# A ninth lasting place for expert weights, and a gather by slot rows with transposes, in a one-core decoder block

## The reference

```python
h = rmsnorm(x, g_pre_ffn) * (1.0 + sc2) + sh2          # (256, 2048)
_, gsel = top_k(h @ w_group + b_group, 1)
pe = softmax((h @ w_router + b_router).reshape(T, 4, 8)[chosen group])
topv, topi = top_k(pe, 2)                              # two experts a token
for every expert e:                                    # w_gate, w_up (2048, 512), w_down (512, 2048)
    hid = silu(h @ w_gate[e]) * (h @ w_up[e])
    y = y + (hid * cw[:, e]) @ w_down[e]
x = x + gt2 * rmsnorm(y, g_post_ffn)
```

## Time and profile before

| | |
|---|---|
| median of 3 runs | 1552.59 us (1552.22 to 1553.93) |
| profiled execution: time, span | 1551.45 us, 1549.6 us |
| PE, DVE, ACT, POOL busy | 97%, 46%, 19%, 3% of the span |
| DMA engines, mean rate over the span | 381 GB/s |
| granted TensorE clock, mean | 0.996 of full speed |

### The profile page before, as it was taken

How to read it: one execution, slowest core, us unless ns; L and a number is a source line. 1 busy time by engine, 2 the same in 40 slices (tenths; PEclk the granted TensorE clock), 3 DMA queues, 4 the chain that set the end, 5 groups by cost and what they waited for, 6 DMA issues and landing times.

```text
span 1549.6 us, 19402 instructions
## 1 busy us (share of the span) xinstructions
PE 1509.9 (97%) x7980; PEld 811.3 (52%) x7980; DVE 714.8 (46%) x1289; ACT 289.9 (19%) x520; POOL 39.8 (3%) x57
## 2 busy tenths in 40 slices
PE   5999999999999999999999999999999999999996
PEld 2888888855654446344344444434434434434432
DVE  3574767676887636243233333332332332432325
ACT  2100311121332303111111112112012112112113
POOL 1001000000001200000000000000000000000003
PEclk9999999999999999999999999999999999999998
DMA  9999777799878996999999999999999999999994
GB/s 363 396 385 367 265 261 283 268 360 353 319 277 314 363 411 250 401 405 425 429 428 427 430 429 427 430 429 427 428 429 428 429 428 428 428 429 428 428 429 194
DMA packets 102802, 589.96 MB, mean 381 GB/s; under 512 B 6224, under 2 KB 16944, under 8 KB 77408
## 3 DMA queue, kind: packets, MB, share of 16 engines
q1 hardware_dynamic: 100384, 580.93, 92.4%
q0 software_dynamic: 1696, 5.66, 1.1%
q10 hardware_dynamic: 672, 2.66, 0.4%
HBM read 587.07 MB, written 2.16 MB: 380 GB/s over the span
## 4 chain that ended last, share of the span: by engine, by line
PE 82%; DMA 14%; DVE 2%; issue 0%; ACTq 0%; SPq 0%; ACT 0%; DVEq 0%
PE bank L1092 24%; DMA ring<-in_w_up 12%; PE bank L1203 11%; PE bank L930 7%; PE bank L646 7%; PE bank L1064 6%; PE bank L680 5%; PE bank L1084 5%; PE bank L871 4%; DMA ring<-in_w_ada 2%; PE bank L714 2%; PE bank L693 1%; PE bank L696 1%; DMA ring<-in_w_in 1%; PE bank L1100 1%; PE bank L837 1%
## 5 line engine op out<-in xcount | busy, mean ns | idle before, releaser
L1092 PE MATMUL bank<-ring,RN 128*64 128x512 f32 x1520 | 333.8, 593 | 3.7 <-DMA ring<-in_w_up 3.6
L1092 PEld LDWEIGHTS bank<-ring,RN 128*64 128x64 f32 x1520 | 108.4, 137 | 221.4 <-issue 208.7
L1203 PE MATMUL bank<-ring,RN 128*64 128x512 f32 x992 | 219.7, 595 | 1.0 <-issue 1.0
L1203 PEld LDWEIGHTS bank<-ring,RN 128*64 128x64 f32 x992 | 68.9, 137 | 137.8 <-issue 136.0
L2219 DVE COPY RG<-bank 64x512 f32<-64x512 f32 x64 | 44.1, 689 | 194.9 <-PE bank L1203 187.2
L1064 PEld LDWEIGHTS bank<-RN,RX 128*128 128x128 f32 x976 | 111.5, 192 | 13.0 <-issue 13.0
L1064 PE MATMUL bank<-RN,RX 128*128 128x128 f32 x976 | 115.7, 277 | 0.0
L930 PE MATMUL bank<-ring,RT 128*128 128x512 f32 x256 | 113.0, 596 | 0.8 <-DVE RT L2000 0.8
L1084 PE MATMUL bank<-RG,RN 128*128 128x512 f32 x240 | 109.5, 599 | 0.0
L2149 DVE TENSOR_SCALAR RN<-bank,aff 128x128 f32<-128x128 f32 x256 | 87.3, 403 | 47.6 <-PE bank L1064 45.7
L2205 DVE TENSOR_TENSOR RN<-bank,RN 128x512 f32<-128x512 f32 x32 | 22.1, 691 | 179.5 <-PE bank L1092 179.5
(11 more groups left out here) (387 smaller groups left out, 1488.0 us busy)
## 6 DMA issues: line engine op xcount, KB each, us to landing
ring<-in_w_down SPq DMA_DIRECT2D x64, 2048.0 KB, 15.5
ring<-in_w_up SPq DMA_DIRECT2D x63, 2048.0 KB, 21.0
ring<-in_w_ada SPq DMA_DIRECT2D x32, 2048.0 KB, 10.8
ring<-in_w_gate SPq DMA_DIRECT2D x32, 2048.0 KB, 19.7
ring<-in_w_in SPq DMA_DIRECT2D x18, 2048.0 KB, 9.3
RH<-in_w_gate SPq DMA_DIRECT2D x16, 2048.0 KB, 21.8
RT<-in_w_gate SPq DMA_DIRECT2D x16, 2048.0 KB, 18.9
ring<-in_w_ada SPq DMA_DIRECT2D x48, 512.0 KB, 11.7
```

The source lines that it names most:

```text
L1092: last = mm(bank[n // 2][c:c + CAP, :], tokT[:, k, q * CAP:(q + 1) * CAP], w[:, i, :], start=k < 2, stop=k >= KT - 2, skip_group_check=True)
L1203: last = mm(bank[2 + n % 2][64 * (n // 2):64 * (n // 2) + 64, :], hidT[:, k * CAP:(k + 1) * CAP], wdn[:, n * BLK:(n + 1) * BLK], start=k = ...
```

## The change

It does two things together.

1. **Memory.** `RN`, `RG[:, 1, :]`, `wide` and `RG[:, 0, :]` become parts of one tile `body`, side by side, so that the last 1024 columns of `RN`, `RG1` and `wide` are one place of 4096 columns. It is the third entry of `ODD`, for piece 2 of odd experts, for the whole loop. `AHEAD` now holds piece 3 of expert 1. Routing numbers move to the constants' tile and to `vec`, the recurrent heads' outputs to `RT[:, 8:16]`. The broadcast of the gate row moves from POOL's queue to SP's, after the third piece of the last expert is used.
2. **The gather.** `gather_rows(p, m)` takes `onehot` as weights and 512 columns of `x_t` as the moving operand, which leaves a bank with slots on the partitions. ACT copies the bank to one row buffer `slot_rows`, `gathered_T(p, m)` transposes it with four transposes into another bank, and DVE's `tokens` reads that. Expert 1's pair is still gathered in the old form.

The diff, cut to its core:

```diff
-        ODD = [blocks_of(RT[:, 0:KT, :].rearrange("p a b -> p (a b)")), blocks_of(RH[:, :])]
+        ODD = [blocks_of(RT[:, 0:KT, :].rearrange("p a b -> p (a b)")), blocks_of(RH[:, :]), blocks_of(body[:, 4096:8192])]
...
+        ROWS_BANK, TOKEN_BANK = [4, 5, 6, 7], [4, 5, 6, 4]
...
-            for s in (1, 0, 2, 4, 3, 5):
+            for s in (1, 0, 2):
+                first_piece(s)
             wait(sp, "rows_sent", 16 * 8)
             wait(sp, "x_permuted1")
...
+            first_piece(4)
+            wait(sp, "gate2_out", 16)
+            sp.dma_start(odd[2], expert_halves(1)[2]).then_inc(sig("odd_landed2").sem, 16)
+            for s in (3, 5):
+                first_piece(s)
+            used(sp, ("out", 3, 1))
...
+            sp.wait_ge(sig("expert_used").sem, (NE - 1) * HB + 3)
+            sp.dma_start(RG1[:, :], late_rows[3 * KT:4 * KT, :].rearrange("(o k) p -> o (k p)", o=1).to_broadcast([P, D]))\
+                .then_inc(sig("gain2_in").sem, 16)
...
+            def gather_rows(p, m):
+
+                if m == 3:
+                    pe.wait_ge(sig("ohwT_copied").sem, p + 1)
+                for tt in range(TT):
+                    last = mm(bank[ROWS_BANK[m]][:, :], onehot[:, tt, :], x_t[:, tt, m * BLK:(m + 1) * BLK], start=tt == 0, stop=tt == TT - 1)
+                last.then_inc(sig("rows_gathered").sem, 1)
+
+            def gathered_T(p, m):
+
+                pe.wait_ge(sig("rows_in_slots").sem, p * 4 + (m + 1))
+                if m == 3:
+                    pe.wait_ge(sig("gathered_used").sem, p * 4 + 5)
+                for j in range(4):
+                    last = tr(bank[TOKEN_BANK[m]][:, j * P:(j + 1) * P], slot_rows[:, j * P:(j + 1) * P], ident)
                 last.then_inc(sig("gathered").sem, 1)
...
-                        for m in range(3):
-                            gather_part(p + 2, m)
-                    if q == 1:
+                        for m in range(2):
+                            gather_rows(p, m)
                         pe.wait_ge(sig("ohw").sem, p + 1)
...
+                        gather_rows(p, 2)
...
                     if q == 1:
-                        gather_part(p + 2, 3)
+                        gathered_T(p, 0)
+                        gather_rows(p, 3)
+                        gathered_T(p, 1)
...
                         if k % 2 == 1:
                             last.then_inc(sig("expert_used").sem, 1)
+                            if q == 1:
+                                gathered_T(p, 2 + k // 2)
...
+            def slots_in(p, m):
+
+                act.wait_ge(sig("rows_gathered").sem, p * 4 + (m + 1))
+                if m:
+                    act.wait_ge(sig("gathered").sem, p * 4 + (m + 4))
+                fn(slot_rows, bank[ROWS_BANK[m]][:, :], ACT.Copy).then_inc(sig("rows_in_slots").sem, 1)
...
-                    if q == 1 and gather_next:
-                        tokens(p + 2, range(3))
...
-                        tokens(p + 2, range(3, 4))
+                        tokens(p + 2, range(4), TOKEN_BANK)
```

More of the change, by code:

```diff
@@ L499, in _, with first_pieces @@
             sp.dma_start(odd[0], expert_halves(1)[0]).then_inc(sig("odd_landed0").sem, 16)
-            def first_halves(e, q):
+            def first_pieces(e, q):
                 pieces = expert_halves(e + 2)
-                for s in range(2):
+                for s in range(3):
                     sp.wait_ge(sig("expert_used").sem, e * HB + (s + 1))
@@ L1053, in _, with gather_last_part @@
             keep_clock(8, 7)
[L1056 to L1062, removed]
+            def gather_last_part():
+                wait(pe, "gathered_used", 1)
+                for k in range(12, 16):
                     for tt in range(TT):
-                        last = mm(bank[GB[m % 3]][:, (k % 4) * P:(k % 4 + 1) * P], x_t[:, tt, k * P:(k + 1) * P],
+                        last = mm(bank[GB[0]][:, (k % 4) * P:(k % 4 + 1) * P], x_t[:, tt, k * P:(k + 1) * P],
                                   onehot[:, tt, :], start=tt == 0, stop=tt == TT - 1)
+                last.then_inc(sig("gathered").sem, 1)
+            def gather_rows(p, m):
[10 more added lines that the diff above has]
+                    last = tr(bank[TOKEN_BANK[m]][:, j * P:(j + 1) * P], slot_rows[:, j * P:(j + 1) * P], ident)
                 last.then_inc(sig("gathered").sem, 1)
@@ L1155, in pair @@
                     for n in range(4):
-                        if n == 2 and ahead:
+                        if n == 3 and ahead:
                             wait(pe, "ahead_landed", 16)
[L1158 to L1161, removed]
+                        elif n == 3 and first:
+                            wait(pe, "expert_landed3", 16)
+                        elif n == 3:
+                            pe.wait_ge(sig("expert_landed3").sem, e * 16)
                         elif q == 0:
@@ L1165, in pair @@
                             pe.wait_ge(sig(f"odd_landed{n}").sem, p * 16 + 16)
-                        w = AHEAD if ahead and n == 2 else ODD[n] if q == 1 and n < 2 else ring[:, n, :, :]
+                        w = AHEAD if ahead and n == 3 else ODD[n] if q == 1 and n < 3 else ring[:, n, :, :]
                         for m in range(2):
@@ L1493, in _ @@
             second_norm(0)
-            wait(act, "rows_sent", 16 * 8)
             x2T_copies(0)
@@ L1520, in expert_act @@
                 fn(sil[64:128, :], hid[0:64, :], ACT.Silu).then_inc(sig("silu").sem, 1)
+                if q == 1 and not last:
+                    slots_in(p, 0)
                 if q == 1:
@@ L1526, in expert_act @@
                    ACT.Copy).then_inc(sig("half_copied").sem, 1)
+                if q == 1 and not last:
+                    for m in range(1, 4):
+                        slots_in(p, m)
                 act.wait_ge(sig("expert_used").sem, e * HB + (5 if last else 6))
@@ L2142, in onehot_pair, with tokens @@
                 last.then_inc(sig("onehot").sem, 1)
-            def tokens(n, ms=range(4)):
+            def tokens(n, ms, banks):
                 for m in ms:
@@ L2163, in _ @@
             step(v.reduce_sum(rt[:, 200:201], rt[:, 0:64], AX), "over_counted")
-            tokens(1, range(3, 4))
+            tokens(1, range(3, 4), FIRST_BANK)
             for tt in range(TT):
```

121 lines of the change are left out of this document (58 added, 63 removed).

## The result

| | before | after |
|---|---|---|
| median of 4 runs each | 1552.4 us (1551.03 to 1553.93) | 1578.54 us (1577.36 to 1579.73) |
| profiled execution: time, span | 1551.45 us, 1549.6 us | 1579.73 us, 1577.5 us |

The ratio is 1.0169, with a 95% interval from 1.0156 to 1.0182: the change costs 26.1 us. Forecast were 1582 us and a range from 1570 to 1592.

The account below looks back on a forecast made before the run. PE's own work plus 5.4 us of weight waits was taken to bound the expert stage. Fifteen pairs at +2.31 us (+34.7) less 5.4 gave +29.3 on 1551.45, 1580.7; with 1.1 for the median, 1582 us, range 1570 to 1592.

Parts of the forecast that it names:

- What bounds the kernel: Expert stage: PE's own work, 57.08 us a pair against the DMA's 58.7, plus 5.4 us of waits for weights.
- The ninth place: Extra weight place in the expert stage: wins back all of PE's waits for weights, 5.4 us in total.
- The gather: Odd experts' gather on PE: 16 wide records take 7.07 us instead of 7.34, -0.27 us a pair.
- Transposes: Sixteen new 128x128 transposes a pair on PE, 0.12 us each; groups 0 and 1 add 0.94 us.
- The trips: Groups 2 and 3, in and behind the down product: leaving half-array work and returning costs 0.35 us each.
- The handoffs: Waits between PE's transposes and ACT's copies into the one row buffer: hidden, booked 0, at most 1.0 us a pair.
- The broadcast: Gate row's load moved to SP's queue in expert 31: hidden by 6 us, booked at 0.
- The last token part: DVE's last token part, now behind the down product: ready by about 2 us, needed 5.2 us into the next blocks.
- The free trip: Rival: changing array halves around the down product costs nothing, +1.61 us a pair, 1571 us; chance 16%.
- the exposed handoffs: Rival: ACT's copies before the transposes hold PE up to 1.0 us a pair, 1587 to 1597 us; chance 13%.
- the transposes' other price: Rival: the gather's transposes cost the skill's price, 4.4 instead of 1.9 us a pair, near 1619 us; chance 1%.
- The faster one: Rival: PE's growth does not appear in the pairs, below 0.36 us each; 1547 us with no growth; chance 5%.

Follow-up runs that it names:

- e2: The kernel before with only the new gather put in and eight places kept: 1577.32 us, ratio 1.016.
- e4: The kernel after with each transpose of the gather made twice into the same place: 1602.78 us, one run.
- e1: The kernel after with the old gather, so the ninth place alone: 1551.39 us, ratio 0.9993 to the kernel before.
- e6: The kernel after with the old gather and, from expert 16 on, two first loads held back instead of three: 1550.36 us, ratio 0.9989 to the kernel before.
- e3: The kernel after with the transposes of group 2 moved ahead of the down product: 1573.09 us, 5.45 us less than after.
- e5: The kernel after with the last gather part moved behind group 1's transposes, leaving ACT's copy uncovered: 1590.95 us, one run.
- e8: Like e6, but with its held-back load order from expert 2 on instead of 16: 1559.34 us, ratio 1.0048 to the kernel before.
- e7: Like e6, but with the gate row's broadcast sent one piece later, after expert 31's fourth block: 1551.1 us, ratio 0.9993 to the kernel before.

## Why the prediction was right, and what in it was wrong

**What bounds the kernel.** Right for the change: PE's 57.1 us a pair stood against 58.7 of the DMA engines, and once PE's own work was 59.14 it paid for every added instruction and waited for none. e2 and e4 show it from two sides. My sentence that "the stage ends when PE has done its own work plus 5.4 us" was a sum that fits, not a cause: in the kernel before, the last loads bound the end, and the 5.4 us are what PE lags because of them, not what more room would win back.

**The ninth place, -5.4: right in size, wrongly attributed.** The waits are gone after, as booked, and for the reason in the second half of my sentence, that PE is then the slower of the two. But "This is worth at most the 5.4 us of waits. I book all of it" ties them to the place. By e2 they go without it; with the old gather the place brings 1.3 us in e1's medians, which is within the noise, and some 2.3 in e6's profile. That the term came out right is luck as far as the place goes: with a growth of PE too small to make it the slower of the two, part of the waits would be left. No run shows that case. I put 9.8 us into the hole, and 7.3 were gained there; missing was what gives them back: 4.9 us when the places are full sooner, and 3.5 us at the switch of the order. I had read the order of the queue only up to the first experts, and the switch at expert 16 is a rule of it that the change touches.

**The gather, -0.27:** -0.37. A quarter as many records at four times the price each, as read; between full-array work it lacks the 0.09 that the scatter's second group has at its border, which is now paid at group 1. The Trainium skill has a figure (TensorE: Matmul & The Clock Gate, Back-to-back issue gap) by which, as an estimate, the gather would have dropped to about 2 us. This trace does not agree: 16 fp32 records take 6.97.

**Transposes, 0.12 each:** 0.11, in the timeline and in e4's pairs. The Trainium skill (TensorE: Matmul & The Clock Gate, PE-mode transpose) gives about 275 ns for one in a kernel's context, by which sixteen would be, as an estimate, 4.4 us. The trace does not agree: four groups take 2.15.

**The trips, 2 x 0.35:** real, as e3 shows, and a little too dear in the forecast. Both cost the same: group 2's is 0.29 by e3, and group 3's is 0.15 over the 0.44 of four transposes, 0.09 in the product ahead and 0.05 in the blocks behind, 0.29 too. The 0.35 was added up from leftovers under 0.12 each. With 0.17 less for groups 2 and 3, 0.10 less for the gather and 0.03 more for groups 0 and 1 the pair grows by 2.07 instead of 2.31, 3.7 us less in fifteen.

**The sum.** 1582 and 1578.5 are 3.5 us apart, but that this looks like the pairs' 3.7 is chance. By the profiles the change is +31.0 in the pairs, -4.3 and -1.95 behind: 24.7 us, where I forecast 29.3. The missing 4.6 are the 3.7 and the 0.9 at the last scatter, which I did not have in the sum. The medians say 26.1; those of e2, compared on its own chip, say 24.65. The 1.4 us between the profiles' sum and the medians are not explained by the loop; ahead of expert 1 single executions differ by up to 3 us (last section).

**The handoffs, 0:** right, with 0.9 us of spare for 0.7 forecast; e5 shows what the cover hides. **The broadcast, 0:** right: after, PE has no wait in expert 31. **The last token part:** right; the next even expert ran its blocks without a wait.

**The rivals.** The free trip (1571) is refuted by e3's pairs, the exposed handoffs by the timeline and e5, the transposes' other price by e4's pairs. The faster one (PE's growth does not appear) needed less than 0.36 us a pair and got 2.07.

## What to carry to other kernels

Where two resources run within 3% of each other, work out two ends, that of the engine's work and that of the last arrival (bytes by rate, plus each pause of the queue). The sum of the waits is not what more room would bring: here it was 5.4 us, and the room brought 2.3 at most. A buffer more pays only as far as the order of the loads leaves no new pause, and a pause with a full store is not free: e8 paid for it 350 us later. Put full-array transposes next to other full-array work: inside a half-array product the same four cost 0.29 us more. And where medians come from different chips, compare the repeating stretch in the profiles, start to start.

## What the runs showed of the hardware

- **The granted clock moves the head of an execution.** The profiled execution of after is 3.2 us late at expert 1 already, ahead of any gather by rows. In the window from 60 to 105 us its granted clock is 0.92 of full speed as a mean, where the kernel before and e1 have 1.00. From 70 to 75 us it is 0.50, the lower of the two levels (1.2 instead of 2.4 GHz); just before, from 65 to 70, PE was busy for 4.0 of 5 us. That it isn't the code two pairs of runs show. e4 is the kernel after up to its first gather by rows: with 1.00 there (and PE busy for 4.4 of the 5 us) it starts expert 1 at 644.23. And e6 and e7 are alike up to their last load: e6 with 1.00 starts expert 1 at 644.36, e7 with 0.92 at 647.16. The windows of after:

```profile
60.00:105.00 45.00, 44.01 (x217) 39.36 (x216) 29.79 (x34) 5.60 (x11) 0.00 (x0) 0.92 1.04 400
...
70.00:75.00 5.00, 5.00 (x15) 4.19 (x15) 1.54 (x8) 3.53 (x6) 0.00 (x0) 0.50 1.01 397
```

- **Borders are not alike.** Four transposes take 0.44 us between full-array work (844.71 to 845.15), 0.53 ahead of half-array ones (846.87 to 847.40) and 0.59 between two half-array groups (850.98 to 851.57).
- **A handoff from PE to ACT and back takes 0.85 us** with a copy of 128x512 (0.60) in it.
